# A gather's two halves waited for apart, and the last token half normed, transposed and stored in column halves

## The chip, the core and the metric

The kernel runs on one core of a Trainium2 chip. TensorE (PE) multiplies matrices, and its weight loads have rows of their own (PEld); VectorE (DVE), ScalarE (ACT) and GpSimd (POOL) do the elementwise work, and SyncE (SP) issues nearly all DMAs. Each engine works through its own list in order, and semaphores tie the lists together. The metric is the device time of one execution in microseconds (us), as the median of several runs.

## The reference, cut to what matters

Two decoder layers over 256 tokens of width 1024, in float32. Per layer:

```python
sh1, sc1, gt1, sh2, sc2, gt2 = split(silu(c) @ w_ada[l] + b_ada[l], 6)
u = x * (1 + sc1) + sh1
proj = u @ w_in[l]                     # q, k, v, o, two gates per head, three conv inputs
h = head_norm(mlstm_chunkwise(q, k, v, i, f)) * sigmoid(o)
y_conv = cb * causal_conv3(cc * ch)
mix = concat(h, y_conv) @ w_out[l]
x = layer_norm(ALPHA * x + (1 + gt1) * mix, ln1_g[l], ln1_b[l])
u = x * (1 + sc2) + sh2
# 4 groups of 4 experts: best group, then the two best experts in it
y = sum_e comb[:, e] * ((silu(u @ w_gate[e]) * (u @ w_up[e])) @ w_down[e])
x = layer_norm(ALPHA * x + (1 + gt2) * y, ln2_g[l], ln2_b[l])
```

## The kernel before, in words

The tokens stand on the 128 partitions in two halves, t = 0 and t = 1: `X[:, t, :]` is 128 tokens by 1024 columns. `uT` holds the modulated input transposed, in eight chunks kc of 128 columns. Weights come in units of 2 MB through six `ring` slots and one more, `bench`; SP issues a unit's load once the last reader of its slot has signalled (`released`). The order of the units and their slots are worked out ahead of time; every engine's list is written out by hand, so the order of the code is the order of the work.

**Output projection and first norm.** PE multiplies `mixT` with `w_out` in four blocks of 128 tokens by 512 columns (L828), in the order (t, half) = (0,0), (1,0), (0,1), (1,1), each into PSUM bank 2t + half, and counts `mix_done` up after each. Every block is 16 instructions of 512 columns in the trace, since a float32 `matmul` of the code is two of the machine. DVE takes a block in `add` (L1161 to L1164: multiply by the gate row, add ALPHA times x, `bn_stats`), then for a token half `moments` (L1168, L1169), `centre` (L1173), a short Newton step with ScalarE's 1/sqrt (L1056 to L1062) and `finish` (L1178), which writes `X[:, t, :]` and counts `x_ready`. Between `moments(1)` and `centre(1)` DVE also makes the shift and scale of the second modulation (`moe_shift_scale`, L1136, L1137), for which it waits on `moe_ext`.

PE meanwhile, after the last block, runs four sums (L536), transposes t = 0 (L581), transposes four columns of the sums (L543), which counts `moe_ext`, fills in twelve matmuls on zeros (`stay_busy`, L504), and transposes t = 1 once `x_ready` says so. ScalarE and DVE modulate the transposed chunks into `uT` (L923, L1049): of t = 1 ScalarE takes chunks 0 to 3 and DVE 4 to 7. The routing logits follow (`in_quarters`, L594), DVE ranks and picks experts, and `build_disp` makes the 0/1 matrix `disp` that sorts tokens into 64 places per expert.

**Experts.** They run in eight pairs. For a pair PE gathers its tokens (`gather`, L634) with eight chunks of x into banks 6 and 7; `xg_half` on ScalarE modulates chunks 0 to 3 from bank 6 (L938) and counts `xg_act`, and on DVE chunks 4 to 7 from bank 7 (L1227) and counts `xg_dve`. Then come `gate_up` for the gate (h = 0 reads chunks 0 to 3 with one ring slot, h = 1 chunks 4 to 7 with the next, L647), the gather of the next pair, `gate_up` for up, the transpose of the hidden values (L655) and down (L671). Each half of a `gate_up` releases a slot. In pair 0 PE waits for both counts at the gate; for the pairs after it waits for both already ahead of L662, in the pair before.

**Last norm and store.** `last_norm` does the same for both halves from the banks that the experts' sum has filled (L1103 to L1118). After layer 0 its `x_ready` starts the transposes of layer 1 (L581, with `stay_busy` between the halves); after layer 1 SP stores each half of 128 by 1024 (L408).

## Time and profile before

| | us |
|---|---|
| median of 3 runs | 835.89 |
| lowest and highest run | 835.6, 835.93 |
| the profiled execution | 835.82 |
| its span, first to last instruction | 834.1 |
| busy PE, PEld, DVE, ACT in the span | 795.4, 419.0, 418.3, 101.3 |
| moved by DMA | 299.29 MB, a mean of 359 GB/s |

The span stands 1.7 us below the time of the same execution. PE is busy for 95% of the span. The two layers take nearly the same course: what stands at 170 to 210 us in layer 0 stands at 569 to 609 us in layer 1. A stretch is read by the chain of waits and then by the timeline of the engines there.

### The profile page before, as it was taken

What the parts mean: (1) busy time and instruction counts of PE and PEld (TensorE: products, weight loads), DVE (VectorE), ACT (ScalarE), POOL (GpSimd) and SP (SyncE); (2) the same over time, 40 slices, a digit from 0 to 9 for tenths busy, and PEclk for the clock granted to TensorE, in tenths of its full rate; (3) what the DMA queues carried; (4) which work ended last, traced back from release to release, by engine and by line L of the source; (5) the groups of instructions that cost most, each with busy time, mean ns of one, the idle gap of its engine ahead of it and who ended that gap; (6) DMA issues with size and microseconds to landing.
All of it is one profiled execution on the core that took longest, in us unless ns stands there. A gap on an engine that the chain in (4) does not pass through costs nothing.

```text
span 834.1 us, 9198 instructions
## 1 busy us (share of the span) xinstructions
PE 795.4 (95%) x3779; PEld 419.0 (50%) x3801; DVE 418.3 (50%) x869; ACT 101.3 (12%) x237; POOL 29.1 (3%) x72
## 2 busy tenths in 40 slices
PE   8999999999999999999979999989899999999994
PEld 3575588445344434444347658844444434443431
DVE  0189888974423332332265985676533332333135
ACT  2111000023011001101111100002311101110110
POOL 3000000620000000000010000000000000000000
PEclk9999999999999999999999999999999999999998
DMA  9998998997999999999999699366699999999991
GB/s 317 389 387 315 388 388 328 362 380 297 390 412 414 415 411 413 415 411 412 411 388 337 224 359 386 140 248 255 226 383 411 414 415 409 415 416 409 414 391 57
DMA packets 90654, 299.29 MB, mean 359 GB/s; under 512 B 4153, under 2 KB 4441, under 8 KB 82417
## 3 DMA queue, kind: packets, MB, share of 16 engines
q1 hardware_dynamic: 86960, 291.60, 90.2%
q0 software_dynamic: 2592, 7.04, 2.2%
q8 instruction: 32, 0.52, 0.3%
q10 hardware_dynamic: 1056, 0.03, 0.1%
q14 instruction: 14, 0.11, 0.0%
HBM read 297.60 MB, written 1.05 MB: 358 GB/s over the span
## 4 chain that ended last, share of the span: by engine, by line
PE 85%; DMA 6%; DVE 4%; issue 3%; ACT 1%; POOL 1%; POOLq 0%; DVEq 0%; ACTq 0%
PE bank L647 22%; PE bank L603 17%; PE bank L671 12%; PE bank L634 8%; PE bank L620 7%; PE bank L828 7%; DMA ring<-in_w_up_dram 6%; PE bank L693 4%; PE bank L504 2%; PE bank L514 1%; PE bank L581 1%; PE bank L655 1%; PE bank L701 1%; ACT uT L923 1%; PE bank L531 0%
## 5 line engine op out<-in xcount | busy, mean ns | idle before, releaser
L603 PE MATMUL bank<-uT,ring 128*128 128x256 f32 x640 | 140.4, 380 | 0.0
L603 PEld LDWEIGHTS bank<-uT,ring 128*128 128x128 f32 x640 | 121.0, 190 | 19.6 <-issue 3.6
L647 PE MATMUL bank<-ring,qT 128*64 128x512 f32 x448 | 99.4, 594 | 2.8 <-issue 2.8
L671 PE MATMUL bank<-ring,hb 128*64 128x512 f32 x448 | 99.6, 595 | 1.4 <-ACT hb L949 1.4
L647 PE MATMUL bank<-ring,uT 128*64 128x512 f32 x448 | 99.2, 593 | 1.1 <-DMA ring<-in_w_up_dram 1.1
L1073 DVE SCALAR_TENSOR_TENSOR bench<-ring,cond,bench 128x512 f32<-128x512 f32 x126 | 94.7, 752 | 4.5
L1248 DVE SCALAR_TENSOR_TENSOR kT<-bank,share,gate_row 128x512 f32<-128x512 f32 x32 | 24.0, 749 | 90.0 <-PE bank L671 90.0
L634 PEld LDWEIGHTS bank<-ccT,X 128*128 128x128 f32 x512 | 61.5, 197 | 13.2 <-issue 11.4
L634 PE MATMUL bank<-ccT,X 128*128 128x128 f32 x512 | 64.6, 285 | 0.2
L647 PEld LDWEIGHTS bank<-ring,uT 128*64 128x64 f32 x448 | 31.6, 137 | 63.9 <-issue 60.2
L647 PEld LDWEIGHTS bank<-ring,qT 128*64 128x64 f32 x448 | 32.2, 137 | 61.7 <-issue 60.8
L671 PEld LDWEIGHTS bank<-ring,hb 128*64 128x64 f32 x448 | 30.9, 137 | 62.8 <-issue 60.5
L1235 DVE TENSOR_TENSOR o_sig<-o_sig,bank 128x512 f32<-128x512 f32 x16 | 11.0, 688 | 100.5 <-issue 80.4
L620 PE MATMUL bank<-ring,uT 128*128 128x512 f32 x128 | 57.5, 608 | 0.0
L828 PE MATMUL bank<-ring,mixT 128*128 128x512 f32 x128 | 55.5, 594 | 1.5 <-ACT mixT L992 1.5
L828 PEld LDWEIGHTS bank<-ring,mixT 128*128 128x128 f32 x128 | 24.2, 190 | 31.6 <-issue 29.7
L693 PE MATMUL bank<-expo,hb 128*128 128x512 bf16 x154 | 37.8, 379 | 2.2 <-issue 2.2
L620 PEld LDWEIGHTS bank<-ring,uT 128*128 128x128 f32 x128 | 24.6, 194 | 30.5 <-issue 30.5
L1227 DVE TENSOR_SCALAR uT<-bank,mod 128x128 f32<-128x128 f32 x32 | 10.9, 404 | 55.0 <-PE bank L634 55.0
L945 ACT ACTIVATE o_sig<-bank 128x512 f32<-128x512 f32 x16 | 9.6, 597 | 218.5 <-PE bank L647 218.5
L504 PE MATMUL bank<-zeros 128*128 128x512 bf16 x88 | 26.9, 449 | 7.5 <-issue 4.5
L1227 DVE TENSOR_SCALAR qT<-bank,mod 128x128 f32<-128x128 f32 x32 | 10.9, 404 | 42.3 <-PE bank L634 42.3
(252 smaller groups left out, 646.4 us busy)
## 6 DMA issues: line engine op xcount, KB each, us to landing
ring<-in_w_gate_dram SPq DMA_DIRECT2D x28, 2048.0 KB, 17.6
ring<-in_w_up_dram SPq DMA_DIRECT2D x28, 2048.0 KB, 17.8
ring<-in_w_down_dram SPq DMA_DIRECT2D x28, 2048.0 KB, 16.0
ring<-in_w_ada_dram SPq DMA_DIRECT2D x24, 2048.0 KB, 18.4
ring<-in_w_in_dram SPq DMA_DIRECT2D x14, 2048.0 KB, 17.7
ring<-in_w_out_dram SPq DMA_DIRECT2D x4, 2048.0 KB, 14.9
bench<-in_w_gate_dram SPq DMA_DIRECT2D x4, 2048.0 KB, 10.1
bench<-in_w_up_dram SPq DMA_DIRECT2D x4, 2048.0 KB, 17.8
```

What stands on the lines that cost most here:

```text
L504: pe.matmul(bank[bk][:, :], zeros[:, 0:P], zeros[:, :], start=True, stop=True)
L603: last = pe.matmul(bank[4 + (b0 + q) % 4][:, 0:SEQ], w[:, kc, q * P:(q + 1) * P], uT[:, kc, :], start=(kc == 0), stop=(kc == KC - 1))
L620: last = pe.matmul(bank[4 + (b0 + t) % 4][:, :], uT[:, kc, t * P:(t + 1) * P], w[:, kc, :], start=(kc == 0), stop=(kc == KC - 1))
L634: last = pe.matmul(bank[6 + kc // 4][:, (kc % 4) * P:(kc % 4 + 1) * P], X[:, t, rows_of(kc)], disp[b][:, t, :], start=(t == 0), stop=(t == ...
L647: last = pe.matmul(bank[bk][CAP * j:CAP * (j + 1), :], xg[b][:, 4 * h + k, CAP * j:CAP * (j + 1)], ring[s[h]][:, 4 * j + k, :], start=(h = ...
L671: last = pe.matmul(bank[6 + half][CAP * j:CAP * (j + 1), :], hhT[:, f, CAP * j:CAP * (j + 1)], ring[s[h]][:, 4 * j + 2 * i + half, :], sta ...
L693: last = pe.matmul(bank[2 * t + half][:, :], sent[b][:, t * P:(t + 1) * P], dn_parts[i][:, half * COLS:(half + 1) * COLS], start=False, st ...
L828: last = pe.matmul(bank[2 * t + half][:, :], mixT[:, kc, t * P:(t + 1) * P], w[:, kc, :], start=(kc == 0), stop=(kc == KC - 1))
L1073: ins = dve.scalar_tensor_tensor(out=sums, in0=w[:, kc, :], scalar=cond[:, kc, 0:1], in1=sums, op0=ALU.mult, op1=ALU.add)
L1227: last = dve.tensor_scalar(xg[b][:, kc, :], bank[7][:, (kc - 4) * P:(kc - 3) * P], mod[:, 3, kc:kc + 1], mod[:, 2, kc:kc + 1], ALU.mult, A ...
L1235: dve.tensor_tensor(hh, sg, bank[5][:, :], ALU.mult).then_inc(S.hh, 1)
L1248: dve.scalar_tensor_tensor(out=dn[:, cols], in0=bank[6 + half][:, :], scalar=share[:, 0:1], in1=gate_row[:, cols], op0=ALU.mult, op1=ALU.m ...
```

## The change

Four edits, apart from what carries them (a new semaphore `half_ready`, room for four `bn_stats` per token half, and SP's count of `mix_done`, which is now five a layer):

- **The gate of a pair.** PE waits for `xg_act` ahead of h = 0 and for `xg_dve` ahead of h = 1, where it waited for both ahead of h = 0.
- **The last output block.** Block (1,1) is made in two pieces of 256 columns, the second in the free half of bank 7; DVE adds each piece as it comes. `bn_stats` is taken over 256 columns everywhere in the first norm.
- **The last finish.** `finish(1)` of both norms is two instructions of 512 columns; the first counts `half_ready`, the second `x_ready`. PE transposes in an order that takes four chunks of the first half and then four of the second, each after its own wait. At the start of layer 1 the matmuls on zeros between the token halves are four, not five.
- **The last store** is two DMAs of 128 by 512 columns.

```diff
@@ SP @@
-                eng.wait_ge(mix_done, 4 * l + 2 * i + 2)
+                eng.wait_ge(mix_done, 5 * l + (2, 5)[i])
...
+        def out_pieces(t, half):
+            if t == 0 or half == 0:
+                return [(bank[2 * t + half][:, :], slice(0, COLS))]
+            return [(bank[3][:, 0:SEQ], slice(0, SEQ)), (bank[7][:, 0:SEQ], slice(SEQ, COLS))]
+        by_half = [c for half in range(2) for c in range(KC) if c // 2 % 2 == half]
+        in_halves = [(slice(0, COLS), half_ready), (slice(COLS, D), x_ready)]
...
-            for t in range(T):
-                sp.wait_ge(x_ready, 2 * T * (DEPTH - 1) + T + t + 1)
-                sp.dma_start(out[0, t * P:(t + 1) * P, :], X[:, t, :]).then_inc(stored, 16)
-            sp.wait_ge(stored, 16 * T)
+            sp.wait_ge(x_ready, 2 * T * (DEPTH - 1) + T + 1)
+            sp.dma_start(out[0, 0:P, :], X[:, 0, :]).then_inc(stored, 16)
+            for cols, done in in_halves:
+                sp.wait_ge(done, 2 * DEPTH if done is half_ready else 2 * T * DEPTH)
+                sp.dma_start(out[0, P:SEQ, cols], X[:, 1, cols]).then_inc(stored, 16)
+            sp.wait_ge(stored, 16 * 3)
@@ PE @@
-                pe.wait_ge(ready, value)
-                for kc in range(KC):
-                    last = pe.transpose(bank[2 * t + kc // 4][:, (kc % 4) * P:(kc % 4 + 1) * P], X[:, t, cols(kc)], ident[:, :])
-                    if kc % 4 == 3:
+                for i, kc in enumerate(order):
+                    if i % 4 == 0:
+                        pe.wait_ge(*ready[i // 4])
+                    last = pe.transpose(bank[2 * t + i // 4][:, (i % 4) * P:(i % 4 + 1) * P], X[:, t, cols(kc)], ident[:, :])
+                    if i % 4 == 3:
                         last.then_inc(xT_ready, 1)
...
-                pe.wait_ge(main.xg_act, n + 1)
-                pe.wait_ge(main.xg_dve, n + 1)
-                gate_up(4, b, s[0:2], lambda i: expert_arrived(pe, l, i, p), main.gate)
+                def here(i):
+                    pe.wait_ge((main.xg_act, main.xg_dve)[i], n + 1)
+                    expert_arrived(pe, l, i, p)
+                gate_up(4, b, s[0:2], here, main.gate)
...
-                    for t in range(T):
-                        transpose_half(t, x_ready, 2 * T * l - T + t + 1, straight)
-                        if t == 0:
-                            stay_busy(5, 5)
+                    transpose_half(0, [(x_ready, 2 * T * l - T + 1)] * 2, straight, range(KC))
+                    stay_busy(4, 5)
+                    transpose_half(1, [(half_ready, 2 * l), (x_ready, 2 * T * l)], straight, range(KC))
...
-                        for kc in range(KC):
-                            last = pe.matmul(bank[2 * t + half][:, :], mixT[:, kc, t * P:(t + 1) * P], w[:, kc, :],
-                                             start=(kc == 0), stop=(kc == KC - 1))
-                        last.then_inc(mix_done, 1)
+                        for to, cols in out_pieces(t, half):
+                            for kc in range(KC):
+                                last = pe.matmul(to, mixT[:, kc, t * P:(t + 1) * P], w[:, kc, cols],
+                                                 start=(kc == 0), stop=(kc == KC - 1))
+                            last.then_inc(mix_done, 1)
...
-                transpose_half(1, x_ready, 2 * T * l + 2, rows_of)
+                transpose_half(1, [(half_ready, 2 * l + 1), (x_ready, 2 * T * l + 2)], rows_of, by_half)
@@ ScalarE and DVE, modulate_half @@
-                for kc in chunks:
+                for i in chunks:
+                    kc = by_half[i] if which else i
@@ DVE, finish of both norms @@
-                    dve.scalar_tensor_tensor(out=X[:, t, :], in0=X[:, t, :], scalar=rstd[:, t:t + 1],
-                                             in1=ln_b[:, :], op0=ALU.mult, op1=ALU.add).then_inc(x_ready, 1)
+                    for cols, done in ([(slice(0, D), x_ready)], in_halves)[t]:
+                        dve.scalar_tensor_tensor(out=X[:, t, cols], in0=X[:, t, cols], scalar=rstd[:, t:t + 1],
+                                                 in1=ln_b[:, cols], op0=ALU.mult, op1=ALU.add).then_inc(done, 1)
@@ DVE, add of the first norm @@
-                    link(dve.bn_stats(stats[:, t, half, :], X[:, t, cols]))
+                        for q in range(ours.start // SEQ, ours.stop // SEQ):
+                            last = dve.bn_stats(stats[:, t, q, :], X[:, t, q * SEQ:(q + 1) * SEQ])
+                    link(last)
```

PE's list after the last output block, layer 0, before (names are tiles with their buffer numbers; what an instruction waits for stands in brackets; x8 is a count of instructions of the code):

```order
L543 MATMUL bank6<-ident,expo 128x128 [waits moe_copied]
L543 MATMUL bank6<-ident,expo 128x128 x3
L504 MATMUL bank5<-zeros 128x512 x12
L581 MATMUL bank2<-ident,X 128x128 [waits x_ready]
L581 MATMUL bank2<-ident,X 128x128 x3
L581 MATMUL bank3<-ident,X 128x128 x4
L587 MATMUL bank6<-zeros 128x256 [waits mod_moe_ready]
```

and after:

```order
L556 MATMUL bank6<-ident,expo 128x128 [waits moe_copied]
L556 MATMUL bank6<-ident,expo 128x128 x3
L517 MATMUL bank5<-zeros 128x512 x12
L595 MATMUL bank2<-ident,X 128x128 [waits half_ready]
L595 MATMUL bank2<-ident,X 128x128 x3
L595 MATMUL bank3<-ident,X 128x128 [waits x_ready]
L595 MATMUL bank3<-ident,X 128x128 x3
L601 MATMUL bank6<-zeros 128x256 [waits mod_moe_ready]
```

The transposes of t = 1 wait twice, once for each column half; the columns of the sums and the filling ahead of them stand where they stood.

PE's list at the gate of pair 0 in layer 0, before and after (`qT` is the gathered and modulated input of this pair):

```order
L878 MATMUL bank<-ident,pmax 1x128 [waits pmax_ready,gate_row_ready]
L647 MATMUL bank<-ring,qT 64x512 [waits landed1,xg_dve,xg_act]
L647 MATMUL bank<-ring,qT 64x512 x7
L647 MATMUL bank<-ring,qT 64x512 [waits landed2]
L647 MATMUL bank<-ring,qT 64x512 x7
```

```order
L894 MATMUL bank<-ident,pmax 1x128 [waits pmax_ready,gate_row_ready]
L661 MATMUL bank<-ring,qT 64x512 [waits landed1,xg_act]
L661 MATMUL bank<-ring,qT 64x512 x7
L661 MATMUL bank<-ring,qT 64x512 [waits landed2,xg_dve]
L661 MATMUL bank<-ring,qT 64x512 x7
```

The wait for DVE's half moved from the first to the second half of the gate.

DVE's list in the first norm of layer 0, from the end of `finish(0)` on, before and after:

```order
L1161 TENSOR_TENSOR tmp<-bank,gate_row 128x512 [waits mix_done]
L1162 SCALAR_TENSOR_TENSOR X<-X,tmp 128x512 [waits dve_step]
L1164 BN_STATS stats<-X 128x6 [waits dve_step]
L1168 BN_AGGR mv<-stats 128x2 [waits dve_step]
L1169 TENSOR_SCALAR var<-mv 128x1 [waits dve_step]
L1136 TENSOR_TENSOR mod<-bank,b_ada_col 128x8 [waits moe_ext]
```

```order
L1181 TENSOR_TENSOR tmp<-bank,gate_row 128x256 [waits mix_done]
L1182 SCALAR_TENSOR_TENSOR X<-X,tmp 128x256 [waits dve_step]
L1185 BN_STATS stats<-X 128x6 [waits dve_step]
L1181 TENSOR_TENSOR tmp<-bank,gate_row 128x256 [waits mix_done]
L1182 SCALAR_TENSOR_TENSOR X<-X,tmp 128x256 [waits dve_step]
L1185 BN_STATS stats<-X 128x6 [waits dve_step]
L1190 BN_AGGR mv<-stats 128x2 [waits dve_step]
L1191 TENSOR_SCALAR var<-mv 128x1 [waits dve_step]
L1155 TENSOR_TENSOR mod<-bank,b_ada_col 128x8 [waits moe_ext]
```

Three instructions of DVE became six of half the width, and the wait for `moe_ext` still stands behind them.

## Rows read from the trace of the kernel before

**Rows 1.** The chain of waits, in order of time: start us, us, engine, work.

```profile
70.77 13.93 PE bank L620 x32
...
117.54 27.64 PE bank L603 x128
...
150.42 27.73 PE bank L828 x64
...
182.92 1.29 DVE X L1178
184.26 1.24 PE bank L581 x8
185.53 1.38 DVE uT L1049 x4
...
196.77 1.40 issue
...
467.87 15.63 PE bank L620 x32
...
595.56 1.40 issue
```

**Rows 2.** Timeline 194 to 199 us: start, us, engine, line, op [idle before <-releaser].

```profile
194.82 1.50 ACT L938 ACTIVATE qT<-bank,mod 128x128 f32<-128x128 f32 x4
...
196.50 0.27 PE L878 MATMUL bank<-ident,pmax 128*1 128x128 f32 x1
196.70 1.37 DVE L1227 TENSOR_SCALAR qT<-bank,mod 128x128 f32<-128x128 f32 x4 [2.04 <-PE bank L634]
...
198.17 7.09 PE L647 MATMUL bank<-ring,qT 128*64 128x512 f32 x32 [1.40 <-issue]
```

**Rows 3.** Timeline at 805 us, PE waits for the last up weights.

```profile
805.07 3.65 PE L647 MATMUL bank<-ring,uT 128*64 128x512 f32 x16 [0.84 <-DMA ring<-in_w_up_dram]
```

**Rows 4.** SP's timeline at 201 us, and a window: DMA share and GB/s are last.

```profile
201.86 0.37 SPq L352 DMA_DIRECT2D ring<-in_w_gate_dram  x1
...
200.00:202.00 2.00, 2.00 (x12) 0.78 (x10) 0.87 (x3) 0.00 (x0) 0.00 (x0) 1.00 0.00 0
```

**Rows 5.** Timeline 178 to 188 us, end of the first norm of layer 0.

```profile
178.19 0.69 DVE L1161 TENSOR_TENSOR tmp<-bank,gate_row 128x512 f32<-128x512 f32 x1 [1.14 <-PE bank L828]
...
180.14 0.64 PE L543 MATMUL bank<-ident,expo 128*128 128x128 f32 x4
...
180.62 0.15 DVE L1169 TENSOR_SCALAR var<-mv 128x1 f32<-128x1 f32 x1
...
180.82 0.17 DVE L1136 TENSOR_TENSOR mod<-bank,b_ada_col 128x8 f32<-128x8 f32 x1
...
187.04 0.63 PE L594 MATMUL bank<-uT,w_route_sb 128*20 128x128 f32 x16 [0.34 <-DVE uT L1049]
...
187.73 0.42 DVE L1408 COPY convT<-bank 128x256 f32<-128x256 f32 x1 [0.84 <-PE bank L594]
```

**Rows 6.** Timeline 431 to 434 us, start of layer 1.

```profile
431.77 1.04 PE L581 MATMUL bank<-ident,X 128*128 128x128 f32 x8
...
432.41 1.51 ACT L923 ACTIVATE uT<-bank,mod 128x128 f32<-128x128 f32 x4 [1.58 <-PE bank L581]
...
432.85 1.37 DVE L1049 TENSOR_SCALAR uT<-bank,mod 128x128 f32<-128x128 f32 x4 [0.23 <-PE bank L581]
```

**Rows 7.** Timeline at the end, and the window with the last store's bytes.

```profile
827.41 3.63 SPq L408 DMA_DIRECT2D out_dram<-X  x2
...
829.38 1.28 DVE L1118 SCALAR_TENSOR_TENSOR X<-X,rstd,ln_b 128x1024 f32<-128x1024 f32 x1
...
832.00:833.00 1.00, 0.00 (x0) 0.00 (x0) 0.00 (x0) 0.00 (x0) 0.00 (x0) 0.50 0.84 332
```

**Rows 8.** Window at 469 us: PEclk stands third from the end.

```profile
469.00:470.00 1.00, 1.00 (x2) 0.33 (x1) 1.00 (x4) 0.28 (x1) 0.00 (x0) 0.53 0.98 367
```

**Rows 9.** The page's groups of instructions: weight loads of float32.

```profile
L828 PEld LDWEIGHTS bank<-ring,mixT 128*128 128x128 f32 x128 | 24.2, 190 | 31.6 <-issue 29.7
```

More of the change, by code:

```diff
@@ L1045, in modulate_half @@
             def modulate_half(l, which, t, chunks):
[L1047 to L1049 removed]
+                for i in chunks:
+                    kc = by_half[i] if which else i
+                    dve.wait_ge(xT_ready, 8 * l + 4 * which + 2 * t + i // 4 + 1)
+                    dve.tensor_scalar(uT[:, kc, t * P:(t + 1) * P], bank[2 * t + i // 4][:, (i % 4) * P:(i % 4 + 1) * P],
                                       mod[:, 2 * which + 1, kc:kc + 1], mod[:, 2 * which, kc:kc + 1], ALU.mult, ALU.add).then_inc(uT_dve, 1)
@@ L1177, in finish @@
                     newton(t, 1, rs_ready, 2 * T * l + t + 1)
-                    dve.scalar_tensor_tensor(out=X[:, t, :], in0=X[:, t, :], scalar=rstd[:, t:t + 1],
-                                             in1=ln_b[:, :], op0=ALU.mult, op1=ALU.add).then_inc(x_ready, 1)
+                    for cols, done in ([(slice(0, D), x_ready)], in_halves)[t]:
+                        dve.scalar_tensor_tensor(out=X[:, t, cols], in0=X[:, t, cols], scalar=rstd[:, t:t + 1],
+                                                 in1=ln_b[:, cols], op0=ALU.mult, op1=ALU.add).then_inc(done, 1)
                 add(0, 0)
```

29 lines of the change are left out of this document (14 added, 15 removed).

## The prediction, made before the changed kernel ran

> **What bounds the kernel now.** I began with the chain of waits, which follows the end of the span back from step to step. For almost all its length it lies on TensorE, and so what matters is where it leaves TensorE: there something late holds the whole kernel. At two kinds of place that this change touches it does. The first is the end of the first norm: the chain goes from VectorE's last `finish` to the eight transposes of t = 1 and then to VectorE's modulation of them [rows 1]. The second is a piece called issue, 1.40 us long and found once in each layer, just ahead of the first gate [rows 1]; here the reader has to open the timeline, since "issue" names no one. It shows TensorE done with its small transpose at 196.77 us, ScalarE's half of the gathered input done at 196.32 (194.82 + 1.50), VectorE's half at 198.07 (196.70 + 1.37), and the gate starting at 198.17 [rows 2]. So the wait is for VectorE's half.
>
> The second view is that of the DMAs, since the experts' weights come at the full rate of the queues from here on, and near the end of the layer TensorE waits 0.84 us for the last weights of up [rows 3]. A gain on TensorE is worth nothing at the end if the stream of weights did not start earlier too. It starts when the first half of the first gate lets its slot go: SP issues that load at 201.86, and from 200 to 202 us the queues moved nothing at all [rows 4]. The stream hangs on the start of the gate, and whatever TensorE gains ahead of it, the stream gains as well.
>
> **The gate's wait.** With the change the first half of the gate needs ScalarE's part only, which is there when TensorE comes at 196.77 us, 1.40 us before the gate started [rows 2]. The second half starts half of 7.09 us after the first, at about 200.3, and VectorE's part has been ready since 198.07; nothing waits there. The wait moved costs at most a tenth where TensorE starts its next group. In the other seven pairs both counts are waited for in the pair ahead, so nothing moves there. Gain: 1.40 a layer, **2.80** in all, with ends at 2.5 and 2.85. Queued behind the gate on TensorE are the next pair's gather and up; both only come earlier, and what they need of VectorE (the next `disp`) is built while the first gate runs, which lasts 7.09 us.
>
> **The last output block.** It looks as if this halves what VectorE has to do behind the last matmul. The block's own time on TensorE stays: 64 rows of 512 columns took 27.73 us, 0.433 each, and 128 rows of 256 columns took 27.64 us, 0.216 each [rows 1], so 32 of the one kind (two pieces of 16) stand for 16 of the other. On VectorE the block takes from 178.19 to the start of `var` at 180.62, with the first instruction 0.69 long [rows 5]. VectorE is free 1.14 us before that block is there, at 177.05 [rows 5]. With the change the first piece has been ready since before 177.05, and VectorE works through six instructions of 256 columns. The trace has one such at 0.42 [rows 5]; with a gap of 0.04, an estimate, six come to 2.76. Of the 2.43 us from 178.19 to 180.62 three instructions of 0.69 with such gaps are 2.19, which leaves 0.24 between the last `bn_stats` and `var`. With 0.10 for the extra `bn_stats` of the block before, `var` starts at 177.05 + 0.10 + 2.76 + 0.24 = 180.15, some 0.45 us earlier than now.
>
> But then comes the wait for `moe_ext`. Now `var` starts at 180.62, and the instruction behind it, which needs no result of it, at 180.82, when TensorE's four columns are done at 180.14 + 0.64 = 180.78 [rows 5]. That chain starts at the end of the last block too, goes through the sums, a copy of ScalarE and eight transposes, and the change leaves it alone. VectorE's 0.45 us become a wait, and `centre(1)` starts when it does now. I take **0.00**, with ends at 0.0 and 0.1 a layer; it would cost something only if the six took 0.45 more than I reckon.
>
> **The last finish and its transposes.** Now 2.61 us pass from the start of `finish(1)` at 182.92 to VectorE's modulation at 185.53, of which 1.29 are the norm's and 1.24 the eight transposes [rows 1]. In two halves the second ends a little later than the whole did. From the rows: one of 1024 columns takes 1.29 [rows 1], one of 512 takes 0.69 [rows 5], so two in a row are 0.09 more at worst, and nothing where they overlap as neighbours without a wait do; I take 0.05. The first four transposes then run under the second half (0.62 us, and 0.6 is there to hide them), and only four, 0.62, remain behind it. Gain: 0.62 - 0.05 = 0.57, less a few hundredths for the second wait: 0.55 a layer, **1.10** in all, with ends at 0.9 and 1.2. Next late is TensorE itself: it waits 0.34 us for VectorE's `uT` at 187.04 [rows 5], and what stands ahead of that wait on TensorE comes 0.55 earlier as well, so that the 0.34 stay.
>
> The Trainium skill has a rule that speaks against all these halves: "Advanced Engine Details and Errata", section "The Read-Write Bubble", asks for tiles of 512 or 1024 elements because each instruction of VectorE shows its memory latency, and "Perfetto Trace Analysis", section "Optimizing Scalar/DVE Operations", puts that at about 60 ns on SBUF. By the rule `finish` in halves would cost 0.06 instead of my 0.05, and the sum would stay as it is to 0.02 us.
>
> **The start of layer 1.** Here the transposes of t = 1 started at 431.77, and the modulation of t = 1 on ScalarE at 432.41 and on VectorE at 432.85, after it stood idle for 0.23 us [rows 6]. VectorE is the last of the two (until 434.22), and it cannot save more than those 0.23; the split `finish` takes 0.05 to 0.09 of them. **0.15**, ends at 0.0 and 0.25. The fifth matmul on zeros that goes makes sure that TensorE is there in time.
>
> **The store.** The last `finish` starts at 829.38 and takes 1.28; the second store is issued as it ends, and SP is done with it at 831.04 [rows 7]. Its bytes still move through 0.84 of the window from 832 to 833 us, at 332 GB/s [rows 7], and 1.1 us later the span is over. Half of the bytes are now gone by the time the last 256 KB are issued: at 332 / 0.84 = 395 GB/s 256 KB are 0.66 us less, and the split `finish` takes 0.05. I take **0.50**, with ends at 0.2 (rows half as long, or two stores in each other's way) and 0.65.
>
> **Sum.** 2.80 + 0.00 + 1.10 + 0.15 + 0.50 = 4.55 us. Against the profiled execution (835.82, span 834.1) that is 831.27 and a span of 829.6; the median stands 0.07 above that execution. Forecast: **831.3**, its own range 830.6 to 832.3. About 0.2%, 1.7 us, is what a measurement of this kernel can tell from no change.
>
> **Rivals.**
>
> *The clock goes another way, and the kernel gets faster still (829.6).* In layer 1 the same 32 matmuls took 15.63 us that took 13.93 in layer 0 [rows 1]. In the window at 469 us the granted clock is 0.53 [rows 8]: TensorE had fallen to its lower level, 1.2 GHz, after small matmuls of four rows, and the same small matmuls in layer 0 did not bring it down. So this fall hangs on where they lie in time, and layer 1 now lies 2.1 us earlier (1.40 + 0.55 + 0.15). If it stays away, 15.63 - 13.93 = 1.70 us more are gained. Against it: nothing in the change touches those matmuls, and the three times before lie within 0.33 us, so the fall comes back in every run. Chance 0.17. The same can happen the other way round: a new fall in a stretch like that costs 1.70, which gives **833.0**, chance 0.08.
>
> The Trainium skill says of this ("TensorE: Matmul & The Clock Gate", section "What's actually happening") that the chip's look at activity runs free and does not begin anew with a kernel; by that rule the 1.70 us would come and go from run to run in either kernel, between 829.6 and 831.3 here, and three times within 0.33 us speak against it.
>
> *The gate's gain does not reach the end (834.1).* Were the stream of weights bound already when the gate starts, TensorE would gain 2.80 and wait it out at the last up, where it waits already [rows 3]. The empty queues at 200 to 202 us speak against it [rows 4]. 831.3 + 2.8 = 834.1, chance 0.04.
>
> *The output block in pieces costs TensorE more than all the rest gives (slower, 843.5).* Each matmul of 256 columns has a weight load of 0.19 us to itself [rows 9], and 32 rows a layer have half the time to hide it. Hidden they cost nothing; left bare they cost 64 x 0.19 = 12.2 us, and 831.3 + 12.2 = 843.5. The point at which it decides is 4.55 / 64 = 0.07 us a row more than 0.216. The 128 rows of the projections with the same loads and 0.216 each [rows 1] speak against it. Chance 0.03.
>
> That the change doesn't do what it says is the case of the output block, and stands in the forecast: its pieces come earlier and nothing follows from it.
>
> **How the numbers follow.** The forecast has 0.68, the faster rival 0.17, the new fall 0.08, the stream 0.04, the slow block 0.03. From 829.5 to 833.1 lie the first three, and the range is that. Faster by over 0.2% are those three together with part of the stream's case, which lies at the edge: 0.93; within 0.2%: 0.04; slower: 0.03.
>
> **What would show it.** The issue of 1.40 us ahead of both first gates is gone, and SP's first load behind the gate comes some 1.95 us earlier in layer 0. The idle time of VectorE ahead of `moe_shift_scale` grows to about half a us, and `centre(1)` starts no earlier against the end of the output block. From the start of `finish(1)` to VectorE's modulation 2.05 us pass instead of 2.61. The last matmuls of 256 columns stand 0.216 apart. The wait for the last up weights stays under 1 us in each layer; had it grown to over 2, the stream was the bound. The prediction is wrong if the fall of the clock at 469 us less the shift is missing, or another stands elsewhere in a stretch of matmuls.

## The result: 829.8 us, within the range, and part of the gain was not the change's

| | before, us | after, us |
|---|---|---|
| median | 835.75 (4 runs) | 829.82 (4 runs) |
| lowest and highest | 835.6, 835.93 | 828.96, 831.42 |
| the profiled execution, and its span | 835.82, 834.1 | 830.04, 828.3 |
| ratio | | 0.9931 (95%: 0.9914 to 0.9948) |

The forecast was 831.3, from 829.5 to 833.1. The changed kernel is 5.9 us faster by the medians, 1.5 us more than forecast, and lies below the forecast's own range (830.6 to 832.3), inside the wider range only by the room that the faster rival had. The number that the runs behind this bear out is another: over all comparisons the kernel before has 65 single times, from 831.1 to 836.33 with a mean of 834.3, and the changed kernel 16, from 827.59 to 831.42 with a mean of 829.9. That is 4.35 us, with a standard error of 0.3. The first four single times of the kernel before lay close together, and high.

The chain of waits of the changed kernel answers to [rows 1]: start us, us, engine, work.

```profile
70.75 13.93 PE bank L634 x32
...
182.94 0.76 DVE X L1201
183.75 1.42 PE bank L595 x8
185.19 1.38 DVE uT L1067 x4
...
192.29 4.04 PE bank L648 x32
196.44 7.02 PE bank L661 x32
```

```profile
466.60 13.93 PE bank L634 x32
```

Nothing called issue stands ahead of the gate any more: the chain goes from the gather at 192.29 straight into the gate at 196.44. (The chain counts the gate from the end of the small transpose, 196.44; the timeline below has its first matmul at 196.37.) The transposes of t = 1 now begin 0.81 us into the last `finish` (183.75 after 182.94). And the 32 matmuls at 466.60 take 13.93 us, as those at 70.75 do, where they took 15.63 in layer 1 before.

Timeline of the changed kernel at the first gate, the counterpart of [rows 2] and [rows 4] (start, us, engine, line, op, operands, and in brackets the idle time ahead and what ended it):

```profile
194.48 1.51 ACT L955 ACTIVATE qT<-bank,mod 128x128 f32<-128x128 f32 x4
...
196.17 0.27 PE L894 MATMUL bank<-ident,pmax 128*1 128x128 f32 x1
...
196.37 1.37 DVE L1250 TENSOR_SCALAR qT<-bank,mod 128x128 f32<-128x128 f32 x4 [2.04 <-PE bank L648]
196.37 7.09 PE L661 MATMUL bank<-ring,qT 128*64 128x512 f32 x32
...
200.06 0.37 SPq L353 DMA_DIRECT2D ring<-in_w_gate_dram  x1
```

ScalarE is done at 195.99, TensorE with its small transpose at 196.44, and the gate starts at 196.37. VectorE's half, for which the gate used to wait, only begins at 196.37 and ends at 197.74. SP's first load behind the gate is issued at 200.06 and not at 201.86.

Timeline at the end of the first norm of layer 0, the counterpart of [rows 5]:

```profile
177.06 0.42 DVE L1181 TENSOR_TENSOR tmp<-bank,gate_row 128x256 f32<-128x256 f32 x1
...
179.98 0.15 DVE L1191 TENSOR_SCALAR var<-mv 128x1 f32<-128x1 f32 x1
...
180.16 0.64 PE L556 MATMUL bank<-ident,expo 128*128 128x128 f32 x4
...
180.84 0.17 DVE L1155 TENSOR_TENSOR mod<-bank,b_ada_col 128x8 f32<-128x8 f32 x1 [0.71 <-PE bank L556]
...
181.00 1.28 DVE L1195 SCALAR_TENSOR_TENSOR X<-X,mv,ln_g 128x1024 f32<-128x1024 f32 x1
...
182.94 1.41 DVE L1201 SCALAR_TENSOR_TENSOR X<-X,rstd,ln_b 128x512 f32<-128x512 f32 x2
...
183.75 1.41 PE L595 MATMUL bank<-ident,X 128*128 128x128 f32 x8 [0.36 <-DVE X L1201]
...
186.71 0.63 PE L608 MATMUL bank<-uT,w_route_sb 128*20 128x128 f32 x16 [0.34 <-DVE uT L1067]
```

`var` starts at 179.98, 0.64 us earlier than before. Then VectorE stands idle for 0.71 us until TensorE's four columns (180.16 + 0.64 = 180.80) release it at 180.84, which is where it was released before (180.82), and `centre(1)` follows at 181.00. The output block's pieces have bought a wait.

**Where the 5.8 us of the span went.** Since the engines work through fixed lists, the span can be cut at the starts of named matmuls of TensorE and compared stretch by stretch. All figures are us, from the profiled execution of each kernel; the names of the experiments are explained below.

| stretch on TensorE | before | after | gate only | finish only | block only | after, 2nd | after, 3rd |
|---|---|---|---|---|---|---|---|
| span's start to gate logits, layer 0 | 37.42 | 37.40 | 36.17 | 35.48 | 35.58 | 35.52 | 37.34 |
| head rows to scores, layer 0 | 15.74 | 15.74 | 15.74 | 15.74 | 15.74 | 17.43 | 15.74 |
| head rows to scores, layer 1 | 17.43 | 15.74 | 15.73 | 15.73 | 17.43 | 15.74 | 17.43 |
| four sums to route logits of t = 1, layer 0 | 8.96 | 8.60 | 8.97 | 8.60 | 8.95 | 8.60 | 8.62 |
| the same, layer 1 | 8.96 | 8.61 | 8.95 | 8.60 | 8.96 | 8.60 | 8.61 |
| those to the first gate, layer 0 | 11.13 | 9.66 | 9.66 | 11.13 | 11.13 | 9.66 | 9.66 |
| the same, layer 1 | 11.13 | 9.66 | 9.66 | 11.13 | 11.13 | 9.65 | 9.67 |
| first gate to the last sum of experts, layer 0 | 221.57 | 221.46 | 221.64 | 221.46 | 221.82 | 222.59 | 221.05 |
| the same, layer 1 | 222.10 | 221.32 | 222.39 | 221.64 | 222.47 | 222.51 | 221.05 |
| that sum to gate logits of layer 1 | 14.77 | 15.42 | 15.35 | 14.59 | 14.68 | 14.58 | 14.57 |
| that sum to the end of the span | 15.04 | 14.79 | 15.03 | 14.78 | 15.01 | 14.83 | 14.81 |

Five rows are the same to 0.05 us in every kernel with the same edit: those of the norm, of the gate and the last. They are the change's own gain: 1.47 + 1.47 at the gates, 0.35 + 0.35 at the norms, and in the last row 0.2 to 0.26 for the store. The others differ between executions of one and the same kernel. In the first pair of profiles they add up to 1.9 us in favour of the change: 1.69 where the clock fell before and not after, 0.89 at the experts, less 0.65 at the start of layer 1.

Of the rows that differ, those of the start of either layer and those behind the head rows follow TensorE's clock, and the experts' rows do not. The first row was the same in the first pair, but over all kernels it moves by 1.9 us: it is 37.3 to 37.4 where the granted clock falls to 0.50 near 8 and again near 22 us, 36.2 to 36.3 where it falls once, near 20 us, and 35.4 to 35.6 where it does not fall. One window of it in the changed kernel, then in the one with `finish` alone:

```profile
22.00:24.00 2.00, 2.00 (x6) 0.60 (x4) 0.00 (x0) 0.00 (x0) 0.00 (x0) 0.50 1.05 387
```

```profile
22.00:24.00 2.00, 1.93 (x17) 0.53 (x18) 0.00 (x0) 0.00 (x1) 0.00 (x0) 1.00 1.04 383
```

The experts' rows follow TensorE's wait for the last weights of up: 221.05 without a wait, 221.47 with one of 0.20 us, 221.57 with 0.30, 222.1 with 0.84 [rows 3], 222.59 with 1.32. The changed kernel's first profile and then its second, which waits once in each layer:

```profile
403.84 3.65 PE L661 MATMUL bank<-ring,uT 128*64 128x512 f32 x16 [0.20 <-DMA ring<-in_w_up_dram]
```

```profile
404.78 3.65 PE L661 MATMUL bank<-ring,uT 128*64 128x512 f32 x16 [1.32 <-DMA ring<-in_w_up_dram]
...
800.83 3.65 PE L661 MATMUL bank<-ring,uT 128*64 128x512 f32 x16 [1.24 <-DMA ring<-in_w_up_dram]
```

Its third profile has no such wait. So this share of the difference is the weights' stream, which comes later or earlier from one execution to the next.

### The profile page after: what moved, and what is told of

The parts are those of the page before. It is cut to its first block, busy times and chain, and to the rows that moved or that the text cites. A ratio compares the mean times of both kernels' runs of the same rounds, so it can differ in the third digit from the quotient of the medians.

```text
span 828.3 us, 9293 instructions
## 1 busy us (share of the span) xinstructions
PE 794.6 (96%) x3810; PEld 424.5 (51%) x3832; DVE 419.6 (51%) x885; ACT 101.4 (12%) x237; POOL 28.8 (3%) x72
## 4 chain that ended last, share of the span: by engine, by line
PE 86%; DMA 6%; DVE 4%; issue 2%; ACT 1%; POOL 1%; DVEq 0%; POOLq 0%; ACTq 0%
PE bank L661 22%; PE bank L617 17%; PE bank L685 12%; PE bank L648 8%; PE bank L844 7%; PE bank L634 7%; DMA ring<-in_w_up_dram 6%; PE bank L707 4%; PE bank L517 2%; PE bank L595 1%; PE bank L527 1%; PE bank L669 1%; PE bank L715 1%; DVE X L1131 1%; PE bank L544 0%
## 5 line engine op out<-in xcount | busy, mean ns | idle before, releaser
L844 PE MATMUL bank<-ring,mixT 128*128 128x512 f32 (+1 forms) x160 | 55.5, 508 | 1.5 <-ACT mixT L1009 1.5
L634 PE MATMUL bank<-ring,uT 128*128 128x512 f32 x128 | 55.8, 594 | 0.0
L844 PEld LDWEIGHTS bank<-ring,mixT 128*128 128x128 f32 x160 | 30.2, 190 | 26.5 <-issue 23.0
## 6 DMA issues: line engine op xcount, KB each, us to landing
bench<-in_w_up_dram SPq DMA_DIRECT2D x4, 2048.0 KB, 17.4
```

Of the source, the lines that this page charges most:

```text
L634: last = pe.matmul(bank[4 + (b0 + t) % 4][:, :], uT[:, kc, t * P:(t + 1) * P], w[:, kc, :], start=(kc == 0), stop=(kc == KC - 1))
L844: last = pe.matmul(to, mixT[:, kc, t * P:(t + 1) * P], w[:, kc, cols], start=(kc == 0), stop=(kc == KC - 1))
```

## The experiments

The theory after the result: the edits are worth about 4 us by themselves, gate and `finish` and store, and the rest is TensorE's clock, which falls at other places in other executions. The rivals: the edits are worth more than I had worked out (the output block among them), or the stream of weights takes part back.

### The parts one by one, and the changed kernel again

The gate's edit alone, on the kernel before:

```diff
-                pe.wait_ge(main.xg_act, n + 1)
-                pe.wait_ge(main.xg_dve, n + 1)
-                gate_up(4, b, s[0:2], lambda i: expert_arrived(pe, l, i, p), main.gate)
+                def here(i):
+                    pe.wait_ge((main.xg_act, main.xg_dve)[i], n + 1)
+                    expert_arrived(pe, l, i, p)
+                gate_up(4, b, s[0:2], here, main.gate)
```

> The kernel before with the edit of the gate's wait alone. Theory (the direct gains are 1.46 us a layer at the gate, 0.34 a layer at the finish, 0.3 at the store, and the rest of the 5.9 us is TensorE's clock: a fall of 1.70 us at 469 us that goes away once layer 1 lies earlier, and another at the start of layer 1 that grows by 0.8): 835.75 - 2.9 = 832.8 where the falls stay as in the kernel before, and 831.1 to 832.0 where the fall at 469 us is gone; the single times differ by 1 to 2 us, and they go with the mean granted clock. Rival A (the edits themselves are worth more than thought, the clock nothing): over 3.5 us gained, 832.2 or less, with the fall at 469 us still there and single times within 0.4 us. Rival B (the stream of weights absorbs part): under 2.2 us gained and a wait for the last up weights of over 1.5 us.

Measured: 830.77 us against 834.79 for the kernel before beside it (23 runs), ratio 0.9959 (0.9944 to 0.9974), which is 3.4 us with 1.3 either way (4.0 by the two medians). The stretch from the route logits to the gate is 9.66 instead of 11.13 in both layers, so 2.94 by the trace. The stream of weights took next to nothing back: TensorE waited 0.38 and 1.12 us for the last weights of up, against 0.30 and 0.84 before, so rival B is out. Rival A's time came (832.2 or less), but neither of its conditions: the fall at 469 us was gone, and the single times ran from 829.59 to 832.04.

`finish(1)`, the transposes of t = 1 and the last store in halves alone (the changed kernel with the gate's two waits ahead of h = 0, the output block whole and `bn_stats` over 512 columns):

```diff
+                pe.wait_ge(main.xg_act, n + 1)
+                pe.wait_ge(main.xg_dve, n + 1)
-                def here(i):
-                    pe.wait_ge((main.xg_act, main.xg_dve)[i], n + 1)
...
-            if t == 0 or half == 0:
-                return [(bank[2 * t + half][:, :], slice(0, COLS))]
-            return [(bank[3][:, 0:SEQ], slice(0, SEQ)), (bank[7][:, 0:SEQ], slice(SEQ, COLS))]
+            return [(bank[2 * t + half][:, :], slice(0, COLS))]
```

> The kernel before with finish(1), the transposes of t = 1 and the last store in halves, and nothing else (gate and output block as before). Theory: 0.34 a layer, 0.1 at the start of layer 1 and 0.3 at the store, about 1.1 us, so 834.7, with the fall of the clock at 469 us still there, since layer 1 has moved by less than half a us. As I predicted it before the result (0.55 a layer and 0.5 at the store) it would be 1.75 us, so 834.0. Rival A: 2 us or more.

Measured: 832.37 us, ratio 0.9981 (0.9968 to 0.9993), 1.6 us with 1.1 either way: the interval can't tell 1.1 from 1.75, nor from rival A's 2. The stretches can: 8.96 became 8.60 in both layers, and the last row 14.78. The fall at 469 us was expected to stay and was gone (15.73). The edits move layer 1 by less than half a us, but in this execution it lay 2.6 us earlier all the same, 1.9 of them from the first row. Its place in time does not decide, though: the head rows of layer 1 stand at 463.31 us here, and at 463.33 in the third profile of the changed kernel, where the clock fell. The window behind them, here and there:

```profile
466.00:467.00 1.00, 1.00 (x3) 0.38 (x2) 0.96 (x5) 0.00 (x0) 0.00 (x0) 1.00 1.03 381
```

```profile
466.00:467.00 1.00, 1.00 (x2) 0.34 (x1) 0.96 (x4) 0.00 (x0) 0.00 (x0) 0.50 1.00 381
```

The output block in two pieces alone, with `bn_stats` over 256 columns:

```diff
-                            last = pe.matmul(bank[2 * t + half][:, :], mixT[:, kc, t * P:(t + 1) * P], w[:, kc, :],
...
+                        for to, cols in out_pieces(t, half):
+                            for kc in range(KC):
+                                last = pe.matmul(to, mixT[:, kc, t * P:(t + 1) * P], w[:, kc, cols],
```

> The kernel before with the last output block in two pieces alone, and bn_stats over 256 columns. Theory: VectorE's var comes 0.6 us earlier and then waits for moe_ext, centre(1) starts when it did, so 835.7 within 0.15 us. Rival (part of the unexpected gain is the block's): 835.2 or less. Rival on the other side (weight loads of the narrower matmuls left bare): 836.5 or more.

Measured: 834.29 us, ratio 0.9997 (0.9984 to 1.0011), against 834.79 for the kernel before beside it. The expected times, 835.7 and 835.2, were reckoned from the first four times of the kernel before and decide nothing here; the ratio and the trace do. Its `var` and what stands behind it in the first norm of layer 0:

```profile
178.16 0.15 DVE L1179 TENSOR_SCALAR var<-mv 128x1 f32<-128x1 f32 x1
...
179.02 0.17 DVE L1143 TENSOR_TENSOR mod<-bank,b_ada_col 128x8 f32<-128x8 f32 x1 [0.71 <-PE bank L549]
```

An idle time of the same length as in the changed kernel, and the stretch behind the block is 8.95 as before. The 32 matmuls of 256 columns start 0.216 us apart, and the stretch that ends with them, from the scores to the four sums, is 93.59 us instead of 93.55. So the pieces bring nothing and cost 0.04 a layer; the rival on the slow side, weight loads left bare, is out as well.

The changed kernel once more:

> The changed kernel once more, for more single times with their clocks. Theory: single times between 828.9 and 831.5 in steps that go with the mean granted clock, 0.987 near 830 to 831.5 and 0.991 near 829 to 829.6, while the kernel before stays within 0.4 us. Rival A: single times spread evenly with the same clock, so the spread is not the clock's.

Measured: 830.92 us, ratio 0.9950 (0.9932 to 0.9968), single times from 827.59 to 831.37. The kernel before ran beside these four, and its 23 single times went from 831.99 to 836.33. So the second half of what I expected was wrong: the kernel before spreads as widely as the changed one. The first half was in part wrong too: the slowest execution here, 831.37, has a mean granted clock of 0.992 and the fastest, 827.59, one of 0.991. The slowest is the profiled one, with the two waits of 1.32 and 1.24 us for weights. Over all 154 single times the mean clock goes with half of the spread (a squared correlation of 0.49 within the groups), not with all of it. In this execution of the changed kernel the clock fell in layer 0, at a place where it had not fallen in the first profiles of either kernel. The windows (PEclk third from the end), and the 32 matmuls in the chain:

```profile
69.00:70.00 1.00, 1.00 (x2) 0.48 (x3) 0.96 (x3) 0.08 (x1) 0.00 (x0) 0.50 1.01 383
70.00:71.00 1.00, 1.00 (x3) 0.48 (x2) 0.96 (x5) 0.10 (x1) 0.00 (x0) 0.50 1.06 414
```

```profile
68.87 15.63 PE bank L634 x32
```

15.63 us instead of 13.93: the same fall and the same price as at 469 us in the kernel before, in the other layer.

### The changed kernel without the pieces

```diff
-            if t == 0 or half == 0:
-                return [(bank[2 * t + half][:, :], slice(0, COLS))]
-            return [(bank[3][:, 0:SEQ], slice(0, SEQ)), (bank[7][:, 0:SEQ], slice(SEQ, COLS))]
+            return [(bank[2 * t + half][:, :], slice(0, COLS))]
...
-                        for q in range(ours.start // SEQ, ours.stop // SEQ):
-                            last = dve.bn_stats(stats[:, t, q, :], X[:, t, q * SEQ:(q + 1) * SEQ])
+                        last = dve.bn_stats(stats[:, t, half, :], X[:, t, ours])
```

> The changed kernel with the last output block whole again and bn_stats over 512 columns. Theory: the pieces bring nothing, since VectorE's list waits for moe_ext behind them; from the sums behind the block to the second half of the route logits 8.60 us pass, as in the changed kernel, and the time is the same as its time within the spread of the clock. Rival: the pieces carry a part; the same stretch takes 8.9 us or more.

Measured: 829.47 us against 834.18 (27 runs), ratio 0.9950 (0.9935 to 0.9966); the stretch behind the block is 8.61 in both layers, as in the changed kernel. The pieces carry no part of the gain.

### The wait that swallows the pieces, moved away

In the changed kernel VectorE waits for `moe_ext` ahead of `centre(1)`, though `centre(1)` needs nothing of it. Here `centre(1)` is issued first:

```diff
-                def centre(t):
-                    link(dve.scalar_tensor_tensor(out=X[:, t, :], ...))
+                def centre(t, then=None):
+                    steps[0] += 1
+                    dve.scalar_tensor_tensor(out=X[:, t, :], ...).then_inc(dve_step, 1)
+                    if then:
+                        then()
+                    dve.wait_ge(dve_step, steps[0])
...
-                moe_shift_scale(l)
-                centre(1)
+                centre(1, lambda: moe_shift_scale(l))
```

> The changed kernel with moe_shift_scale moved: VectorE issues centre(1) first and waits for moe_ext behind it, while centre(1) runs. Theory: the wait for moe_ext is what swallows the output block's pieces; with it out of the way centre(1) starts about 0.85 us earlier, the two small additions cost 0.15 of that behind it, and the stretch from the sums to the route logits falls from 8.60 to 7.9 us in each layer, 1.4 us in all against the changed kernel. ScalarE's modulation of t = 0 starts 0.45 later and could be the next bound; then 8.1. Rival (moe_ext is not the wait that counts): 8.5 or more.

Measured: 828.71 us, ratio 0.9940 (0.9919 to 0.9961). Timeline of layer 0:

```profile
179.94 0.15 DVE L1191 TENSOR_SCALAR var<-mv 128x1 f32<-128x1 f32 x1
...
180.01 1.27 DVE L1196 SCALAR_TENSOR_TENSOR X<-X,mv,ln_g 128x1024 f32<-128x1024 f32 x1
180.12 0.64 PE L556 MATMUL bank<-ident,expo 128*128 128x128 f32 x4
...
181.20 0.16 DVE L1155 TENSOR_TENSOR mod<-bank,b_ada_col 128x8 f32<-128x8 f32 x1
...
184.34 1.37 DVE L1067 TENSOR_SCALAR uT<-bank,mod 128x128 f32<-128x128 f32 x4 [0.94 <-PE bank L595]
...
185.85 0.64 PE L608 MATMUL bank<-uT,w_route_sb 128*20 128x128 f32 x16 [0.26 <-ACT uT L940]
```

`centre(1)` starts at 180.01 and no longer at 181.00, ahead of the columns' end at 180.76, and `moe_shift_scale` runs behind it. The stretch from the sums to the route logits is 7.79 us in layer 0 and 7.81 in layer 1: 0.8 less than in the changed kernel, where 0.7 was expected. The last row also shows what is next: TensorE now waits for ScalarE's part of `uT` by 0.26 us.

With the output block whole:

> As the kernel with moe_shift_scale moved, but with the output block whole. Theory: without the pieces VectorE reaches centre(1) only 0.3 us earlier than in the changed kernel and pays 0.15 for the additions behind it: 8.45 us for the stretch, so that the pieces are worth about 0.5 us a layer once the wait is moved, where they were worth nothing before. Rival: 8.0 or less, so that the move alone does it and the pieces still bring nothing.

Measured: 829.77 us, ratio 0.9950 (0.9934 to 0.9967); the stretch is 8.40 us in both layers. So with the wait moved the pieces are worth 0.6 us a layer, and with the wait in place nothing (8.60 with them, 8.61 without). The move alone brings 0.2.

Both once more beside each other:

> The kernel with moe_shift_scale moved once more, beside the changed kernel on the same chip. Theory: 1.6 us below the changed kernel (twice 0.80), so 5.7 below the kernel before. Rival (the saved time is lost further on): less than 0.8 us below the changed kernel.

> The changed kernel a third time, as the partner of the two others. Theory: its direct gains in the stretches of the trace are 4.0 us (gate 2.94, first norm 0.70, start of layer 1 0.10, end 0.25), so about 4 us below the kernel before; the rest of the first comparison's 5.9 us was the clock's. Rival: 5.5 us or more again.

Measured: 829.26 us with the move (ratio 0.9935, 0.9915 to 0.9956) and 829.71 without (0.9946, 0.9927 to 0.9965), the kernel before 833.99 (11 runs). The medians lie 0.45 us apart, which meets the letter of the rival (under 0.8), but the two intervals overlap and can't tell 0.45 from 1.6; the stretches are 7.79 and 7.82 against 8.61 in both layers, and nothing of the saved time is lost further on (the table of spans below). Over both comparisons the move has 13 single times with a mean of 828.8 and a standard error of 0.3, against 829.9 for the changed kernel: 1.1 us with an error of 0.4, and the 1.6 of the trace is not ruled out by that. It is the fastest kernel that I would keep: by the means beside each other 5.1 and 5.3 us below the kernel before, and 5.6 by the stretches. The changed kernel came out at 4.3 us here, and not at 5.5 or more.

### Filling TensorE's idle time at the start of layer 1

In the first profile of the changed kernel the clock stayed down for longer there than before (it does so with the gate's edit alone too, 15.35 us). Timeline and windows (PEclk third from the end), the counterpart of [rows 6]:

```profile
427.97 1.91 PE L517 MATMUL bank<-zeros 128*128 128x512 bf16 x4
...
429.68 1.87 PE L595 MATMUL bank<-ident,X 128*128 128x128 f32 x8
...
430.78 1.51 ACT L940 ACTIVATE uT<-bank,mod 128x128 f32<-128x128 f32 x4 [1.84 <-PE bank L595]
...
431.58 1.36 DVE L1067 TENSOR_SCALAR uT<-bank,mod 128x128 f32<-128x128 f32 x4 [0.74 <-PE bank L595]
...
433.25 1.05 PE L608 MATMUL bank<-uT,w_gates_sb 128*8 128x256 f32 x16
```

```profile
423.00:424.00 1.00, 0.38 (x1) 0.11 (x2) 1.00 (x2) 0.32 (x2) 0.00 (x0) 1.00 1.05 387
425.00:426.00 1.00, 0.00 (x0) 0.00 (x0) 1.00 (x1) 0.00 (x0) 0.00 (x0) 0.50 1.05 387
429.00:430.00 1.00, 1.00 (x5) 0.55 (x3) 1.00 (x3) 0.00 (x0) 0.14 (x1) 0.50 1.07 393
432.00:433.00 1.00, 0.41 (x2) 0.00 (x0) 0.95 (x3) 0.29 (x1) 0.00 (x0) 1.00 1.05 385
```

At the lower clock the second set of transposes takes 1.87 us, not 1.04, and the whole stretch 15.42 us, not 14.77. The attempt to prevent it:

```diff
-                    stay_busy(2, 5)
+                    stay_busy(10, 5)
```

> The changed kernel with ten matmuls on zeros instead of two at the start of layer 1, while VectorE still norms layer 0. Theory of the clock: TensorE falls to its lower level there because it stands idle behind the experts' sum; with the filling there is no fall between 420 and 435 us in layer 1, and from the last sum of the experts to the gate logits of layer 1 some 14.2 us pass instead of 14.6 to 15.4. Rival: the fall comes all the same (the idle time ahead of the filling is enough), and the filling then runs at half the clock and holds the transposes up: 16 us or more.

Measured: 831.43 us, ratio 0.9969 (0.9950 to 0.9988), single times from 827.7 to 834.16, the widest of all. The clock did not fall there in its profile:

```profile
419.82 2.32 PE L517 MATMUL bank<-zeros 128*128 128x512 bf16 x10
...
424.66 1.09 PE L595 MATMUL bank<-ident,X 128*128 128x128 f32 x8 [2.52 <-DVE X L1137]
...
427.92 2.63 DVE L1067 TENSOR_SCALAR uT<-bank,mod 128x128 f32<-128x128 f32 x8
...
430.86 1.05 PE L608 MATMUL bank<-uT,w_gates_sb 128*8 128x256 f32 x16
```

The stretch took 14.58 us, though, not 14.2. That is what the changed kernel takes too when the clock is up again by the second set of transposes (14.58 and 14.57 in its second and third profile): VectorE's modulations, eight in a row in 2.63 us, set it, and such a fall costs nothing. The same filling on the kernel with the wait moved:

> The kernel with moe_shift_scale moved, and ten matmuls on zeros instead of two at the start of layer 1. Theory: without a fall of the clock there, the stretch from the experts' last sum to the gate logits takes 14.58 us every time, which VectorE sets, against 14.6 to 15.5 with two; that is 0.4 us in the mean and nothing at the least. So the same time as without the filling, within the spread. Rival (the earlier single times of this filling, 831.4 in the middle, were no accident and it costs 1.5 us): the stretch or another one is longer in its profile than in the kernel with two.

Measured: 828.08 us, ratio 0.9933 (0.9912 to 0.9953). Here the profile shows the rival of the run before, and this run's own:

```profile
423.30 4.02 PE L517 MATMUL bank<-zeros 128*128 128x512 bf16 x10 [4.12 <-issue]
...
427.15 1.04 PE L595 MATMUL bank<-ident,X 128*128 128x128 f32 x8
...
431.64 1.05 PE L608 MATMUL bank<-uT,w_gates_sb 128*8 128x256 f32 x16
```

TensorE had stood idle for 4.12 us and the ten matmuls ran at half the clock, 4.02 us instead of 2.32. The transposes came at 427.15 and the stretch took 16.16 us. So filling brought nothing against a fall that is soon over, and cost 1.6 where it ran at the lower clock; at most it could save 0.9, where a fall would have held both sets of transposes, and no run here shows that saving. Whether it costs in the mean can't be settled from these runs: the median of the first kernel with it is 1.4 above that of all 16 times of the changed kernel, none of which ran beside it, and that of the second is 1.2 below its partner's beside it.

## Why the prediction was right, and where it was not

The direct terms add up to about what was forecast, 4.0 us for 4.55; the 829.8 of the first comparison also holds some 1.5 us that are luck, and by the prediction's own last sign (no fall at 469 us less the shift) its account of the clock was wrong.

**The gate (2.80 forecast, 2.94 measured).** Right in place, cause and size: the timeline named the wait that the chain calls issue. The extra 0.07 a layer is this: I counted from the end of the small transpose, and the gate's first matmul starts 0.07 ahead of that end (196.37 against 196.44).

**The stream of weights.** Right: SP's load behind the gate came 1.8 us earlier, and the stretch of the experts is no longer than before, 221 to 222.6 us in all kernels. The wait for the last up, which I had put under 1 us as a sign, was 0.20 us in layer 0 and none in layer 1 of the first profile, but 1.32 and 1.24 in the second and none in the third. That is a spread of executions and not the gate's price: the block-only kernel, without the gate's edit, waits 0.55 and 1.20.

**The output block (0.00 forecast, 0.00 measured).** Right, and for the reason given: `moe_ext`. I had `var` at 180.15 and it came at 179.98, and the idle time at half a us, where it is 0.71. The last matmuls stand 0.216 apart, as I had said. Both sides were shown: alone the pieces do nothing, and behind the moved wait they give 0.6 a layer.

**The last finish (1.10 forecast, 0.70 measured).** The mechanism was right, the size not, and two of its terms failed: from the start of `finish(1)` to VectorE's modulation 2.25 us pass, where I had said 2.05 for 2.61. The split costs 0.13 and not 0.05: two instructions of 512 columns take 1.41 where one of 1024 took 1.28; my bound of 0.09 "at worst" was no bound. And I halved the time of the transposes, 1.24 to 0.62, as if it were all in proportion. From the end of `finish(1)` to VectorE's modulation eight transposes took 185.53 - 184.20 = 1.33 us, and four take 185.19 - 184.35 = 0.84. Four less save 0.49, 0.12 each, and by a straight line through the two figures, an estimate, some 0.35 stay however few they are. 0.49 - 0.13 = 0.36, where the stretch shows 0.35. The 0.06 that stands beside my 0.05 in the prediction is half of the 0.13 measured.

**The start of layer 1 (0.15 forecast, 0.1 to 0.2 measured where the clock is up again by the second transposes).** 14.57 to 14.59 against 14.68 and 14.77. What I left out is that the clock is worth up to 0.9 us there, more than the edit.

**The store (0.50 forecast, 0.25 measured).** The last `finish` and the two stores (SP's row spans both issues), and the windows behind them, the counterpart of [rows 7] (DMA share and GB/s last):

```profile
823.85 1.41 DVE L1137 SCALAR_TENSOR_TENSOR X<-X,rstd,ln_b 128x512 f32<-128x512 f32 x2
824.63 1.05 SPq L421 DMA_DIRECT2D out_dram<-X  x2
```

```profile
825.00:826.00 1.00, 0.00 (x0) 0.00 (x0) 0.27 (x1) 0.00 (x0) 0.00 (x0) 0.50 0.51 188
826.00:827.00 1.00, 0.00 (x0) 0.00 (x0) 0.00 (x0) 0.00 (x0) 0.00 (x0) 0.50 0.90 334
```

The failed term is "half of the bytes are now gone by the time": 0.66 us. The two stores are issued 0.69 us apart, and by the trace's packets bytes move only from 825.48 on, without a gap until 827.48 (188 and 334 KB in the two windows), so the second store's queue behind the first's. Even so the last byte comes 1.80 us after the last issue has ended (825.68), where it came 2.37 after it before: 0.57 less. But the landing is signalled 0.46 us after the last byte, as in all ten profiles with the split store (0.46 or 0.47), where it was 0.27 to 0.30 in the three with one. From the end of the last `finish` (825.26) to the end of the span 3.08 us pass, and 3.45 before. That gives 0.37, of which the split takes 0.13. Why the landing comes later is open.

**The clock, and the rest that differs between executions.** Here the argument failed, though the rival's time came out. I gave 0.17 to a faster kernel at 829.6, on the ground that layer 1 now lies elsewhere against the fall at 469 us; the fall [rows 8] was indeed gone in the first profile of the changed kernel. But it was back in its third (17.43), in the second it was in layer 0, and with `finish` alone it was gone with layer 1 at the same place in time as in the third. Among the thirteen profiles of this case the stretch behind the head rows was slow twice in layer 0 and five times in layer 1, at 17.4 us instead of 15.7, under all kinds of edits. The Trainium skill's statement, that the look at activity runs free and does not start with the kernel ("TensorE: Matmul & The Clock Gate", section "What's actually happening"), agrees with that. I had set it aside because three single times of the kernel before lay within 0.33 us; 65 of them lie within 5.2. Nothing ties the missing fall to the change, and the 829.8 was not the rival's sum either: in the first pair of profiles 1.69 us of clock and 0.89 of weights came on top of the change, and 0.65 of clock went against it. By the single times 1.5 us of the first comparison are no gain of the change. Why the first four times of the kernel before were so close to each other stays open.

That these rows hold the whole difference can be tested on the spans. Take off from each span what the first row has over 35.5, the two rows behind the head rows over 15.74, the two of the experts over 221.05, and the start of layer 1 over 14.58 (over 14.68 without the split `finish`):

| kernel | spans, us | left, us |
|---|---|---|
| before; block only | 834.1; 832.8 | 828.8; 828.9 |
| gate only | 829.1 | 825.9 |
| finish only | 828.7 | 827.7 |
| changed, three profiles; without the pieces; ten on zeros | 828.3, 829.7, 828.5; 826.4; 827.8 | 824.9, 824.9, 824.9; 824.9; 825.0 |
| wait moved, two profiles; ten on zeros | 825.6, 828.2; 825.7 | 823.3, 823.3; 823.3 |
| wait moved, block whole | 828.4 | 824.5 |

The spans in one row lay up to 3.2 us apart, and what is left of them agrees to 0.1. The change is worth 3.9 here, and 4.0 with the 0.1 at the start of layer 1; moving the wait is worth 1.6 more.

The sum of the direct terms by the stretches is 2.94 + 0.70 + 0.1 + 0.25 = 4.0 us, against 4.55 forecast and 4.35 with an error of 0.3 by the single times. So the forecast was right for the change, by terms of which two were 0.3 to 0.4 too high.

## What to carry to other kernels

A wait for two engines ahead of work that reads their results one after the other is worth taking apart, and the timeline tells beforehand what it brings: the distance between the two ends. Work made ready earlier is worth nothing while another wait stands between it and its consumer in the same engine's list; look at the first instruction behind it that waits for another engine, and whether it could stand behind. And where single executions of a kernel spread by 5 us, as 65 of them did here, stretches between named instructions of two traces tell 0.1 us apart that medians of ten runs do not.

## What the runs showed of the hardware that I had not expected

- TensorE's clock fell from 2.4 to 1.2 GHz (granted 1.00, then 0.50) while it worked without a gap, behind a stretch of matmuls with four rows of weights, in seven of 26 passages through that stretch, and each fall cost 1.7 us of 32 matmuls. Two executions that reached the stretch at 463.31 and 463.33 us differed in it.
- Two falls near 8 and 22 us, ahead of layer 0, cost 1.9 us together, and came in five of thirteen profiles.
- A run of ten matmuls on zeros in an idle stretch did not keep the clock up every time: it ran in 2.32 us once and in 4.02 us once.
- Two instructions of VectorE with 512 columns each took 1.41 us in a row, one of 1024 took 1.28; two `bn_stats` of 256 columns took 0.75 and one of 512 took 0.69.
- From the end of its input to its reader a group of eight transposes of 128 by 128 in float32 took 1.33 us, one of four 0.84: 0.12 for each, and by that, an estimate, some 0.35 for the group itself.
- The last byte of two stores of 256 KB issued 0.69 us apart came 0.57 us earlier after the last issue than that of one of 512 KB, and the landing was signalled 0.46 us after it instead of 0.30.
